# A two-layer decoder trunk on one core: early dense tiles for block 0, queries head by head, and one-hot rows scaled by GpSimd

## What is computed

```python
q = (xt @ w_query).reshape(t, PEER_HEADS, 2, PEER_KEY_DIM // 2)          # 8 heads
s1 = jnp.einsum('thd,hnd->thn', q[:, :, 0], sub_keys[0])                 # 128 keys
s2 = jnp.einsum('thd,hnd->thn', q[:, :, 1], sub_keys[1])
v1, i1 = lax.top_k(s1, 16); v2, i2 = lax.top_k(s2, 16)
top_s, sel = lax.top_k(v1[..., :, None] + v2[..., None, :] ..., 16)      # 16 pairs a head
gate = jax.nn.softmax(top_s, axis=-1)
pre = jnp.einsum('td,thkd->thk', xb, expert_u[ib])
act = jax.nn.gelu(pre, approximate=False) * gb
out = jnp.einsum('thk,thkd->td', act, expert_v[ib])
```

## Time and profile before

| | us |
|---|---|
| runs of the kernel, median of 3 | 3512.56 (3504.34 to 3512.86) |
| the profiled execution, its own time | 3508.12 |
| its span, first to last instruction | 3506.3 |
| PE busy in the span | 2561.2 (73%) |
| DVE busy | 2657.0 (76%) |
| ACT busy | 858.1 (24%) |
| POOL busy | 1617.1 (46%) |

### The profile page before, as it was taken

The page is one execution under the profiler, slowest core; times in us unless marked ns, Lnnn a source line. Parts: engine busy times, 40 slices in busy tenths (PEclk is TensorE's granted clock), DMA queues, the critical chain, the costliest instruction groups (busy, mean ns, idle before and its releaser), DMA issues.

```text
span 3506.3 us, 30630 instructions
## 1 busy us (share of the span) xinstructions
PE 2561.2 (73%) x10143; PEld 1712.6 (49%) x10143; DVE 2657.0 (76%) x3661; ACT 858.1 (24%) x1616; POOL 1617.1 (46%) x1028
## 2 busy tenths in 40 slices
PE   7999896602554279999879998966025552799998
PEld 7978785501331054444378887855013310544443
DVE  6776689998888996665167766899988899966663
ACT  5455400005770020000044544000047700200000
POOL 0000146656777726776000000566567777277771
PEclk9999998856776579999989999988557765799999
DMA  5436599988999949999544455999989999499995
GB/s 194 169 136 211 196 360 379 399 356 360 398 408 409 410 147 410 409 406 408 185 134 166 156 192 194 370 375 399 356 359 398 406 411 415 146 409 408 405 409 218
DMA packets 277374, 1111.11 MB, mean 317 GB/s; under 512 B 28440, under 2 KB 40928, under 8 KB 210656
## 3 DMA queue, kind: packets, MB, share of 16 engines
q0 software_dynamic: 147456, 805.37, 57.5%
q1 hardware_dynamic: 129760, 303.78, 24.0%
HBM read 1106.96 MB, written 2.10 MB: 316 GB/s over the span
## 4 chain that ended last, share of the span: by engine, by line
PE 50%; DVE 23%; DMA 10%; issue 7%; POOL 5%; DVEq 4%; ACT 1%; POOLq 0%; SPq 0%; ACTq 0%
PE PS L944 25%; PE PS L573 18%; DVE work L2031 11%; DMA work<-in_peer_u_dram,idx 8%; POOL work L1395 4%; PE PS L892 3%; DVE cst L2088 2%; DVEq L1920 2%; DVE cst L2084 1%; DVE gain L1921 1%; DVE xs L2097 1%; POOL late L1408 1%; DVE gain L1922 1%; DMA late<-in_peer_v_dram,idx 1%; DMA raw<-in_w_in_dram 1%
## 5 line engine op out<-in xcount | busy, mean ns | idle before, releaser
L1395 POOL DMA_INDIRECT work<-in_peer_u_dram,idx x512 | 846.3, 1653 | 1358.5 <-DVEq L1999 860.7
L2031 DVE CUSTOM_DVE_ANT_0 work<-work,hn 128x2048 f32<-128x2048 f32 x512 | 1154.4, 2289 | 95.4 <-DMA work<-in_peer_u_dram,idx 77.4
L1408 POOL DMA_INDIRECT late<-in_peer_v_dram,idx x344 | 509.6, 1481 | 333.4 <-DVEq L2098 238.6
L2097 DVE SCALAR_TENSOR_TENSOR xs<-late,pre,xs 128x1024 f32<-128x1024 f32 x280 | 359.6, 1284 | 187.0 <-DMA late<-in_peer_v_dram,idx 184.6
L937 PE MATMUL PS<-late,work 128*128 128x512 f32 x256 | 206.8, 954 | 218.3 <-DMA late<-in_peer_v_dram,idx 217.4
L1408 POOL DMA_INDIRECT hn<-in_peer_v_dram,idx x168 | 261.0, 1553 | 126.8 <-DVEq L2098 69.9
L573 PE MATMUL PS<-hi,hT_hi 128*128 128x512 f32 (+1 forms) x704 | 273.8, 389 | 2.5 <-DVE lo L1505 2.5
L573 PE MATMUL PS<-hi,hT_lo 128*128 128x512 f32 (+1 forms) x704 | 267.7, 380 | 0.0
L573 PE MATMUL PS<-lo,hT_hi 128*128 128x512 f32 (+1 forms) x704 | 267.6, 380 | 0.0
L1505 DVE TENSOR_TENSOR lo<-raw,hi 128x2048 fp32r<-128x2048 f32 (+1 forms) x60 | 133.3, 2222 | 166.0 <-ACT hi L1028 98.3
L928 PEld LDWEIGHTS PS<-cst 128*128 128x128 f32 x1024 | 178.0, 256 | 138.0 <-DVE cst L2088 66.1
(11 more groups left out here) (328 smaller groups left out, 4339.6 us busy)
## 6 DMA issues: line engine op xcount, KB each, us to landing
late<-in_peer_v_dram SPq DMA_DIRECT2D x128, 512.0 KB, 6.7
hn<-in_peer_v_dram SPq DMA_DIRECT2D x128, 512.0 KB, 6.7
raw<-in_w_in_dram SPq DMA_DIRECT2D x40, 1024.0 KB, 4.7
gain<-in_w_in_dram SPq DMA_DIRECT2D x38, 1024.0 KB, 4.8
raw<-in_w_out_dram SPq DMA_DIRECT2D x16, 1024.0 KB, 5.2
gain<-in_w_out_dram SPq DMA_DIRECT2D x16, 1024.0 KB, 5.2
work<-in_peer_query_dram SPq DMA_DIRECT2D x16, 512.0 KB, 7.1
query_raw<-in_peer_query_dram SPq DMA_DIRECT2D x8, 1024.0 KB, 10.9
```

The costliest lines, as they stand in the source:

```text
L1395: pool.indirect_dma_start(out=urow[r % URING], out_offset=None, in_=experts, in_offset=bass.IndirectOffsetOnAxis(ap=idx[:, b, k:k + 1], ax ...
L1408: pool.indirect_dma_start(out=vrow[r % VRING], out_offset=None, in_=halves_v, in_offset=bass.IndirectOffsetOnAxis(ap=idx[:, b, k:k + 1], a ...
L2031: dve.tensor_tensor_reduce(u, u, hn[:, b, :], 1.0, 0.0, ALU.mult, ALU.add, pre[:, b, r % PICKS:r % PICKS + 1]).then_inc(u_free.sem, 1)
L2097: dve.scalar_tensor_tensor(out=x, in0=vrow[r % VRING], scalar=pre[:, b, k:k + 1], in1=x, op0=ALU.mult, op1=ALU.add)
```

## The change

Constants: `SUMMED` 48 becomes 24; `EARLY` = 24 and `EARLY_RING` = 2 are new. PE multiplies the first 24 tiles for block 0 as soon as block 0's matrix is complete, from the two tile slots that are free then; SP loads them there. In the main pass all 128 tiles are loaded again, and the first 24 are multiplied for block 1 only. 24 V rows of block 0 that PE summed are now added by DVE.

`query(i, half)` goes over the four pieces once for each head, and ACT copies each head's bank by itself; the pieces are released in the second half.

DVE makes both of block 1's one-hot rows of a round with a compare of 128x512 each; POOL multiplies the one by the weights (`scale_hot`), in place, and `build` waits for POOL. POOL fetches six V rows ahead of these multiplies and one after each second one.

The next layer's `split_piece` follows all row adds.

```diff
-SUMMED = 48
+SUMMED = 24
+EARLY = 24
...
+                def load_early(i):
+                    if i >= EARLY_RING:
+                        stop_until(sp, "sp", early_used.sem, early_used.upto(l, i - EARLY_RING + 1))
+                    tile_into(i % EARLY_RING, i)
+
                 def load_tile(i):
                     if i >= TILES:
                         stop_until(sp, "sp", tiles_used.sem, tiles_used.upto(l, i - TILES + 1))
-                    sp.dma_start(vtile[i % TILES].unsqueeze(1),
-                                 peer_v[l:l + 1, i * NKEYS:(i + 1) * NKEYS, 0:DENSE].rearrange("a p n -> p a n")
-                                 ).then_inc(tile_loaded[i % TILES].sem, 16)
+                    elif i < EARLY_RING:
+                        stop_until(sp, "sp", early_used.sem, early_used.upto(l, EARLY - EARLY_RING + i + 1))
+                    tile_into(i % TILES, i)
...
-                load_tile(0)
-                load_tile(1)
+                for i in range(EARLY):
+                    load_early(i)
                 stop_until(sp, "sp", idx_ready.sem, idx_ready.upto(l, GROUPS))
                 next_gain = norm_mix[l + 1:l + 2] if l + 1 < DEPTH else norm_final.unsqueeze(0)
                 sp.dma_start(gain[:].unsqueeze(1), next_gain.partition_broadcast(P)).then_inc(gain_loaded.sem, 16)
+                load_tile(0)
+                load_tile(1)
                 stop_until(sp, "sp", dotted.sem, dotted.upto(l, 2))
...
+                def query(i, half):
+
+                    pe.wait_ge(query_taken.sem, query_taken.upto(l, 2 * i + half))
+                    for q in range(QP):
+                        j = QP * i + QP + q
+                        name = QUERY_BUFFERS[j - QP]
+                        if half == 0:
+                            pe.wait_ge(wq_loaded[name].sem, wq_loaded[name].upto(l, 16 * query_loads(j)))
+                        w = query_landing(j).rearrange("p (c n) -> p c n", c=QC)
+                        for n in range(QC):
+                            c = QC * q + n
+                            for m in (2 * half, 2 * half + 1):
+                                for part in range(2):
+                                    mm = pe.matmul(q_out[:, m, :], w[:, n, m * P:(m + 1) * P], hT[part][:, c, :],
+                                                   start=(c == 0 and m % 2 == 0 and part == 0), stop=(c == NC - 1 and m % 2 == 1 and part == 1))
+                        if half == 1:
+                            mm.then_inc(query_done.sem, 1)
+                    if half == 0:
+                        mm.then_inc(query_even.sem, 1)
...
-                        pe.wait_ge(hot1_ready.sem, hot1_ready.upto(l, n + 1))
+                        pe.wait_ge(hot_scaled.sem, hot_scaled.upto(l, n + 1))
...
-                    for q in range(QP):
-                        query(i, q)
+                    query(i, 0)
                     key_scores(2 * i + 2)
+                    query(i, 1)
                     key_scores(2 * i + 3)
                 turn_picks(0)
                 for n in range(NHOT):
                     build(0, n)
-                    sum_row(n)
-                for r in range(NHOT, SUMMED):
-                    sum_row(r)
+                    if n < SUMMED:
+                        sum_row(n)
+                pe.wait_ge(evicted.sem, evicted.upto(l, NHOT))
+                for i in range(EARLY):
+                    early_landed(i)
+                    dense(i, 0, i % EARLY_RING).then_inc(early_used.sem, 1)
                 turn_picks(1)
                 for n in range(NHOT):
                     build(1, n)
                 pe.wait_ge(evicted.sem, evicted.upto(l, 2 * NHOT))
                 for i in range(NKEYS - TAIL):
                     tile_landed(i)
-                    dense(i, 0)
-                    dense(i, 1).then_inc(tiles_used.sem, 1)
+                    if i >= EARLY:
+                        dense(i, 0, i % TILES)
+                    dense(i, 1, i % TILES).then_inc(tiles_used.sem, 1)
                 for i in range(NKEYS - TAIL, NKEYS):
                     tile_landed(i)
-                    mm = dense(i, 0)
+                    mm = dense(i, 0, i % TILES)
                 mm.then_inc(dense_done.sem, 1)
                 for i in range(NKEYS - TAIL, NKEYS):
-                    dense(i, 1).then_inc(tiles_used.sem, 1)
+                    dense(i, 1, i % TILES).then_inc(tiles_used.sem, 1)
                 if l + 1 < DEPTH:
                     for f in range(4):
...
-                def take_query(i):
-                    act.wait_ge(query_done.sem, query_done.upto(l, QP * i + 2 * QP))
-                    act.activation(qpT[0], bank(6), ACT.Copy)
-                    act.activation(qpT[1], bank(7), ACT.Copy).then_inc(query_taken.sem, 1)
+                def take_query(h):
+                    if h % 2 == 0:
+                        act.wait_ge(query_even.sem, query_even.upto(l, h // 2))
+                    else:
+                        act.wait_ge(query_done.sem, query_done.upto(l, QP * (h // 2) + QP))
+                    act.activation(qpT[h % 2], bank(6 + h % 2), ACT.Copy).then_inc(query_taken.sem, 1)
...
-                for r in range(ahead, V_ROWS):
+                def scale_hot(n):
+
+                    if n == 0:
+                        pool.wait_ge(picks_taken.sem, picks_taken.upto(l, 2))
+                    pool.wait_ge(hot1_ready.sem, hot1_ready.upto(l, n + 1))
+                    ts = slice(BATCH * n, BATCH * (n + 1))
+                    pool.tensor_tensor(hot[:, n % 2, 1], hot[:, n % 2, 1],
+                                       turned_picks[:, 0, ts].unsqueeze(2).to_broadcast([P, BATCH, NKEYS]), ALU.mult
+                                       ).then_inc(hot_scaled.sem, 1)
+
+                for r in range(ahead, ahead + VRING):
+                    fetch_v(r)
+                for n in range(NHOT):
+                    scale_hot(n)
+                    if n % 2 == 1:
+                        fetch_v(ahead + VRING + n // 2)
+                for r in range(ahead + VRING + NHOT // 2, V_ROWS):
                     fetch_v(r)
...
-                    for u in range(BATCH):
-                        t = BATCH * n + u
-                        d = dve.tensor_scalar(hot[:, n % 2, 1, u, :], const("iota"), turned_picks[:, 1, t:t + 1], turned_picks[:, 0, t:t + 1],
-                                              ALU.is_equal, ALU.mult)
-                    d.then_inc(hot1_ready.sem, 1)
+                    dve.tensor_tensor(hot[:, n % 2, 1], bc(const("iota").unsqueeze(1), [P, BATCH, NKEYS]),
+                                      bc(turned_picks[:, 1, ts].unsqueeze(2), [P, BATCH, NKEYS]), ALU.is_equal).then_inc(hot1_ready.sem, 1)
...
-                for r in range(SUMMED + NHOT // 2 + 1, V_ROWS - 16):
+                for r in range(SUMMED + NHOT // 2 + 1, V_ROWS):
                     add_row(r)
                 if l + 1 < DEPTH:
                     split_piece(l + 1, 0)
-                for r in range(V_ROWS - 16, V_ROWS):
-                    add_row(r)
```

More of the change, by code:

```diff
@@ L72 @@
 URING, VRING, TILES = 6, 6, 4
-SUMMED = 48
+SUMMED = 24
+EARLY = 24
+EARLY_RING = 2
 DIAGS = 4
@@ L77 @@
 V_SLOT = [len(range(i, V_ROWS, VRING)) for i in range(VRING)]
-TILE_SLOT = [len(range(i, NKEYS, TILES)) for i in range(TILES)]
+TILE_SLOT = [len(range(i, NKEYS, TILES)) + (EARLY // EARLY_RING if i < EARLY_RING else 0) for i in range(TILES)]
 DENSE = D // 2
@@ L878, in query_odd @@
                     mm.then_inc(query_done.sem, 1)
-                def query(i, q):
-                    j = QP * i + QP + q
-                    name = QUERY_BUFFERS[j - QP]
-                    pe.wait_ge(wq_loaded[name].sem, wq_loaded[name].upto(l, 16 * query_loads(j)))
-                    w = query_landing(j).rearrange("p (c n) -> p c n", c=QC)
-                    if q == 0:
-                        pe.wait_ge(query_taken.sem, query_taken.upto(l, i + 1))
-                    for n in range(QC):
-                        c = QC * q + n
-                        for m in range(4):
-                            for part in range(2):
-                                mm = pe.matmul(q_out[:, m, :], w[:, n, m * P:(m + 1) * P], hT[part][:, c, :],
-                                               start=(c == 0 and m % 2 == 0 and part == 0), stop=(c == NC - 1 and m % 2 == 1 and part == 1))
-                    mm.then_inc(query_done.sem, 1)
+                def query(i, half):
[16 more added lines that the diff above has]
+                        mm.then_inc(query_even.sem, 1)
                 def key_scores(h):
-                    pe.wait_ge(query_taken.sem, query_taken.upto(l, h // 2 + 1))
+                    pe.wait_ge(query_taken.sem, query_taken.upto(l, h))
                     pe.wait_ge(top_taken.sem, top_taken.upto(l, h))
@@ L939, in sum_row, with dense, early_landed @@
                     mm.then_inc(v_summed.sem, 1)
-                def dense(i, b):
+                def dense(i, b, slot):
```

(12 more changed lines are left out.)

11 lines of the change are left out of this document (9 added, 2 removed).

## The result

| | before | changed |
|---|---|---|
| median of the runs, us | 3509.3 (3502.22 to 3513.53, 8 runs) | 3522.26 (3516.9 to 3526.98, 8 runs) |
| the profiled execution, its own time | 3508.12 | 3526.74 |
| its span | 3506.3 | 3524.9 |
| DVE / PE / POOL busy | 2657.0 / 2561.2 / 1617.1 | 2725.7 / 2534.9 / 1669.4 |

The ratio is 1.0036, 95% interval [1.0024, 1.0048]: 13 us slower.

The account below looks back on a forecast made before the run. DVE was taken to bound block 0's U stage and block 1's build, DMA block 1's U stage, PE and DMA both the dense stage; -20 + 0 + 52 - 16 = +16 on 3508.1 gave 3524 us, range 3446 to 3556.

Parts of the forecast that it names:

- Queries, -20: U stage, block 0: head 2's scores come before DVE wants them, 10 us a layer saved, -20 (ends 0 and -22).
- Build, +52: Build of block 1's matrix: 6.31 us a pair of rounds, 1.61 more than now, 26 us a layer (bounds +11 and +84).
- Rival A: Build: GpSimd's multiply and DVE's compares take turns; the forecast itself, 3524 us (3483 to 3556), chance 0.60.
- following each other: Build: DVE's instructions and the multiplies taken one after another, 3.83 + 2 x 1.24 = 6.31 us a pair.
- 5.8 us a pair: Build: pair time over 32 pairs of both layers at which the other gains of 36 us are used up.
- half of that: Build: the earlier rows show POOL waiting for a two-SBUF-input DVE instruction, never DVE waiting for POOL.
- Tiles in the U stage, 0: Block 1's U stage: 24 V rows go and 24 tiles come, same DMA bytes, so 0 (ends -4 and +6).
- the forecast's end of +6: Block 1's U stage: upper end of the early tiles' 0 term, for bunching.
- Rival C: Early tiles outlast the U stage and delay block 1's picks; at 9 us a tile 3598 us, chance 0.07.
- Dense stage, -16: Dense stages: row adds end them, not PE; layer 0 -21, layer 1 +5, together -16 (ends -35 and +10).
- Rival D: Dense stage: DMA carries more than 0.8 transfers a us, so PE ends it at +412; 3470 us, chance 0.03.
- layer 0's gain: Layer 0's dense stage: adds end at +438 instead of +463; with the moved split and shared DMA 442, or -21.

Follow-up runs that it names:

- the PSUM experiment: Changed kernel, with block 1's compares reading the row of key numbers from PSUM, so they have one SBUF input: 3503.83 us, ratio 0.9982 against the kernel before.
- Q: The queries head by head; as the only edit to the kernel before: 3490.39 us, ratio 0.9941.
- T alone: Kernel before with only 24 early tiles and 24 row sums fewer, the split in its old place: 3511.66 us, ratio 1.0001.
- S: The next layer's weight split moved behind all row adds; as the only edit to the kernel before: 3494.28 us, ratio 0.9945.
- Q and S alone: Kernel before with queries head by head and the split behind all row adds, without early tiles or GpSimd's multiply: 3470.81 us, ratio 0.9884.
- G: GpSimd multiplies block 1's one-hot rows and DVE only compares; as the only edit to the kernel before: 3549.76 us, ratio 1.0109.
- ACT versions: Changed kernel with the multiply on ACT, as four scaled copies of 128x128 a round: 3485.55 us, ratio 0.9923 against the kernel before.
- DVE alone: Changed kernel with GpSimd's multiply taken back, DVE comparing and scaling as before: 3489.86 us, ratio 0.9944 against the kernel before.

## Why the prediction was right, and where its working was not

The forecast of 3524 against 3522.26 has the right sign, and the mechanism that decides it, multiply and compares taking turns, is shown. That it is so near is luck: against -20 + 0, +52 and -16 the stages gave -15, +34 and -6, errors of +5, -18 and +10 that add up to -3.

**Queries, -20: right.** By itself the part gave -20, by the stages of one execution -15. DVE's first top-k of head 2 has no wait left; in the earlier trace rows it waited 10.93:

```profile
498.34 0.29 DVE L1969 MAX8 gain<-PS 128x8 f32<-128x128 f32 x1
```

**Build, +52: the mechanism right, the size too large; it is +34.** Rival A, take turns, holds: every experiment with the multiply beside two-operand DVE reads loses, and the one with an operand in PSUM wins half back. Two values were off. The multiply was taken at 1.24 from the fetch that was not held up; it measures 1.05. And "following each other" was applied to all of it: 3.83 + 2 x 1.05 = 5.93 even so, while the pair takes 5.72: the two are not simply added up. POOL's fetch, which the sum left out, lies on the path with 1.41, but two compares run beside it (0.56 + 0.60, and 0.08 until the multiply): without the fetch that stretch would be 1.24, so it costs some 0.2 us a pair. The held multiply and the held compare each overlap a part of what holds them, ending 0.89 and 0.56 after it and not 1.05 and 0.69. The forecast named 5.8 us a pair as the point where the gains are used up and 5.5 as the point under which the kernel is faster by over 0.3%. The pair at 5.72 came with a loss of 13 us, because the gains beside it were 21 and not 36.

The Trainium skill ("SBUF — State Buffer", the section on SBUF's two separate sides) calls the pair of ports an exclusive lock, held for a whole instruction by whichever of DVE, with two SBUF inputs, and GpSimd, reading SBUF, starts first. The forecast could show half of that. The changed kernel's trace agrees with the other half (the compare of 1.33 us), and the PSUM experiment agrees with its condition of two SBUF inputs. The Trainium skill's "GPSIMD Engine Reference" (Performance versus the Vector engine) gave an estimate of 1.12 us for the multiply by scaling 2048 elements down; measured 1.05, it was nearer than the fetch that the sum used. The forecast said that this estimate would make its sum 12 us longer. That is so only with 0.30 us of issue gap added to each; 1.12 in place of 1.24 makes it 64 x 0.12 = 8 us shorter, and the multiplies show gaps of 0.01 to 0.08, no 0.30.

**Tiles in the U stage, 0: right in the whole kernel.** POOL's and SP's bytes are the same, but the U rows that end the chain there now land later: 14 us where it was 9 to 11. Pieces of the chain between 1060 and 1170 us, of before and then of changed:

```profile
1085.81 9.34 DMA work<-in_peer_u_dram,idx
1135.84 9.44 DMA work<-in_peer_u_dram,idx
```

```profile
1069.57 14.09 DMA work<-in_peer_u_dram,idx
1119.91 15.06 DMA work<-in_peer_u_dram,idx
```

The tiles alone came with U stages 5 us a layer longer, 10 in all, past the forecast's end of +6; with Q it cost nothing that shows (781.9 and 781.6 against 780.0 and 781.6). Rival C is out: PE begins the tiles at 1034.30, is through at 1171 (forecast 1160) and waits 45 us for the picks.

```profile
1034.30 5.09 PE L964 MATMUL PS<-late 128*128 128x512 f32 x8 [0.69 <-ACT late L1351]
```

```profile
1216.51 0.48 PE L935 MATMUL PS<-cst,pre 128*128 128x128 f32 x1 [45.44 <-DVEq L2128]
```

**Dense stage, -16: the bound right, both ends forecast too early.** The rows end it, not PE, in both layers, as forecast. But they end at 443.5 and 444.6, not 438, and PE at 423, not 412. Of the first 24 tiles those from the seventh on take 2.56 us each, not 2.3, each with a wait for its tile; all 24 take 63 us, not 55. And the stage's 333 transfers went at 333 / 443 = 0.75 a us, not 0.768:

```profile
1330.27 1.98 PE L964 MATMUL PS<-hn,work 128*128 128x512 f32 x4 [0.55 <-DMA hn<-in_peer_v_dram]
1332.83 1.98 PE L964 MATMUL PS<-hn,work 128*128 128x512 f32 x4 [0.58 <-DMA hn<-in_peer_v_dram]
```

So layer 0 gained 17 in place of 21, and layer 1 lost 11 in place of 5: the sum is -6, not -16. Rival D is out: DMA went at 1.01 to 1.03 already, as before, and PE doesn't end the stage.

**The reason given for layer 0's gain was wrong.** The forecast wrote that "the 16 adds that no longer wait behind the split are what makes this gain". T alone, with the 16 adds behind the split, ends layer 0 at the same 463.9. With 24 more rows on DVE the split, wherever it stands, waits 2.4 us at most for its inputs, so its place means nothing: behind the adds, they end 2 us earlier and the split's 2.3 us follow them. The move gains where PE ends the stage, 25.6 us without the tiles. There the loss is 16 row adds that begin only at 1740.95, after the split that waited 83.15 us. T and S each take away this same loss: T fills the wait with more rows, which also lengthens the rows; S leaves the wait (45.85 us in S alone) but has no adds behind it, at no price that shows. Adding their effects up as if they were independent hid that Q and S alone were the better kernel. The end of layer 0 in the changed kernel:

```profile
1751.40 5.52 DVE L2144 SCALAR_TENSOR_TENSOR xs<-late,pre,xs 128x1024 f32<-128x1024 f32 x4
1757.13 2.29 DVE L1555 TENSOR_TENSOR lo<-raw,hi 128x2048 fp32r<-128x2048 f32 x1 [0.21 <-issue]
```

**By runs.** Q -20, S on top of it -20, T on top of both +19, G on top of all +32. They end at the changed kernel by construction; what they show is each part's size beside the others.

**Left open.** Why a row given back costs 2.3 us in the dense stage rather than the 1.3 of one transfer at 0.768 a us, was not tried separately. The earlier trace rows give an estimate: beside tiles that PE takes at one in 3.44 us, 124 + 62 rows took 389.2 us, 2.1 us a row, which is what the tiles leave; 1.3 would hold only where no tiles are loaded. The faster tile cycle at the stage's start (2.56 us) takes more DMA from the rows and may be the rest, but this is only argued. Tiles and row sums were only ever exchanged one for one; early tiles beside all 48 row sums were not tried. A ring of three one-hot buffers, which the PSUM and ACT versions could use, was not tried.

## What to carry to other kernels

Before moving work from DVE to GpSimd, look at what DVE does meanwhile: where its instructions read two SBUF operands, price the move as if both ran on one engine. One operand in PSUM gave half of the loss back here, and DVE alone was still 14 us better. When two parts of a change take away the same loss, count it once, and ask which of them does so at the lower price. A split of work between PE and DMA-fed rows has a crossing, and here half of the amount in the change was on the right side of it and the whole was not: compute when either side ends as a function of the amount before fixing it.

## What was not expected of the hardware

A DVE compare of 128x512 with an operand in PSUM takes the same 0.69 us as with both in SBUF, and neither waits for GpSimd's multiply nor holds it up (1.05 beside it). The multiply's time is thus 1.5 times the compare's for the same elements, and it goes from 1.05 to 2.01 behind one row add of 1.28.

PE's granted clock in the build fell from 0.72 to 0.57, and the products of a round took 2.07 us for most of it. With compares alone it was 0.93 in the same stage, with a pause of 1.45 us in each pair where the changed kernel has 0.39 and 1.18; what set it is not shown. The lower clock looks like a part of the loss and is none here, since PE isn't in the cycle of 5.72 us. In the PSUM version it is: there a pair whose products took 1.16 us (round at 1237.96) lasted 4.64 us, the pair before, at some 2.1 us a round, 5.54. No run had the changed build with PE at the higher clock throughout.

Tiles and U rows together moved as many bytes as V and U rows did, at 402 GB/s in that stage where it was 401, but the landing of the U rows in the chain went from 9 to 11 us to 13 to 15 while the tiles were loaded. The DMA system, full in both, gave the same total and a different wait to each requester.
